# A hybrid decoder layer with 32 experts: key lengths as logarithms, another router order, ring places released in the mixer, last expert in smaller transfers

## What is computed

```python
h = layer_norm(x, ln0_g, ln0_b)
mix = token_mixer(h, mem, ...)            # projections, gated delta rule, short conv, cross-attention
h = layer_norm(ALPHA * h + mix, ln1_g, ln1_b)
ffn = moe_ffn(h, ...)                     # 32 experts, 4 per token
out = layer_norm(ALPHA * h + ffn, ln2_g, ln2_b)

# in token_mixer, the part of q and k that the change touches
q = l2_normalize(heads(q)) * GDN_HEAD_DIM ** -0.5
k = l2_normalize(heads(k))
o = gated_delta_rule_chunked(q, k, v, g, beta)
o = o * rsqrt(mean(square(o)) + RMS_EPS) * gdn_norm

# in moe_ffn
logits = x @ w_router + b_router
top_logits, top_idx = top_k(logits, 4); top_w = softmax(top_logits)
gate, up = split(x_e @ w_gate_up[e] + b_gate_up[e], 2)    # for the tokens of expert e
gate = min(gate, 7); up = clip(up, -7, 7)
y = ((up + 1) * gate * sigmoid(1.702 * gate)) @ w_down[e] + b_down[e]
out[token] += top_w * y
```

## Time and profile before

| | before |
|---|---|
| median of 3 runs | 1257.62 us |
| the profiled execution's own time | 1255.7 us |
| its span, first to last instruction | 1254.0 us |
| PE busy | 1213.0 us (97%) |
| DVE busy | 390.5 us (31%) |
| ACT busy | 243.5 us (19%) |
| POOL busy | 148.7 us (12%) |
| granted TensorE clock, mean | 0.994 |
| DMA over the span | 453.45 MB, mean 362 GB/s |

### The profile page before, as it was taken

The page is one execution under the profiler, slowest core; times in us unless marked ns, Lnnn a source line. Parts: engine busy times, 40 slices in busy tenths (PEclk is TensorE's granted clock), DMA queues, the critical chain, the costliest instruction groups (busy, mean ns, idle before and its releaser), DMA issues.

```text
span 1254.0 us, 17233 instructions
## 1 busy us (share of the span) xinstructions
PE 1213.0 (97%) x7155; PEld 613.1 (49%) x7155; DVE 390.5 (31%) x768; ACT 243.5 (19%) x402; POOL 148.7 (12%) x106
## 2 busy tenths in 40 slices
PE   8999999999999999999999999999999999999995
PEld 8999999998733333333333333333333333333332
DVE  6675633335522222222222222222222222222224
ACT  5764354544210000000000000000010000000001
POOL 7454323555100000000000000000000000000000
PEclk9999999999999999999999999999999999999999
DMA  9644231875899999999999999999999999999994
GB/s 335 221 148 143 70 136 67 330 292 201 353 409 429 428 429 428 427 429 429 429 428 429 429 429 428 429 428 430 428 429 427 427 427 428 429 427 428 428 427 198
DMA packets 53388, 453.45 MB, mean 362 GB/s; under 512 B 6925, under 2 KB 7002, under 8 KB 28762
## 3 DMA queue, kind: packets, MB, share of 16 engines
q1 hardware_dynamic: 53338, 452.71, 87.0%
HBM read 451.64 MB, written 1.05 MB: 361 GB/s over the span
## 4 chain that ended last, share of the span: by engine, by line
PE 78%; DMA 8%; SPq 5%; DVE 3%; ACT 3%; issue 2%; POOL 0%; DVEq 0%; ACTq 0%
PE bank L1419 29%; PE bank L1491 15%; DMA late<-in_w_gate_up_dram 8%; PE bank L1209 6%; SPq L807 5%; PE bank L1210 5%; PE bank L1211 5%; PE bank L1504 4%; PE bank L1390 4%; PE bank L1405 2%; PE bank L1479 1%; ACT late L1181 1%; ACT w_hi L1069 1%; PE bank L1499 1%; DMA raw<-in_w_mem_kv_dram 0%
## 5 line engine op out<-in xcount | busy, mean ns | idle before, releaser
L1419 PE MATMUL bank<-late 128*64 128x512 f32 x1536 | 343.5, 595 | 5.4 <-DMA late<-in_w_gate_up_dram 5.4
L1491 PE MATMUL bank<-late 128*64 128x512 f32 x1024 | 229.6, 601 | 6.0 <-ACT late L1181 6.0
L1419 PEld LDWEIGHTS bank<-late 128*64 128x64 f32 x1536 | 106.7, 137 | 223.2 <-issue 209.6
L1491 PEld LDWEIGHTS bank<-late 128*64 128x64 f32 x1024 | 71.3, 138 | 142.4 <-issue 128.6
L1209 PE MATMUL bank<-act_hi,w_hi 128*128 128x256 f32 x448 | 129.5, 289 | 1.9 <-DVE early L1699 1.4
L1210 PE MATMUL bank<-act_lo,w_hi 128*128 128x256 f32 x448 | 125.8, 281 | 0.0
L1211 PE MATMUL bank<-act_hi,w_lo 128*128 128x256 f32 x448 | 125.7, 281 | 0.0
L1834 DVE TENSOR_SCALAR late<-bank 128x512 f32<-128x512 f32 x32 | 22.1, 692 | 308.9 <-PE bank L1419 308.9
L1419 PE MATMUL bank<-raw,late 128*64 128x512 f32 x512 | 116.7, 598 | 1.5 <-DMA raw<-in_w_gate_up_dram 1.5
L770 POOL TENSOR_TENSOR w_lo<-raw,w_hi 128x1024 fp32r<-128x1024 f32 x33 | 81.9, 2483 | 102.1 <-ACT w_hi L1069 102.0
L1209 PEld LDWEIGHTS bank<-act_hi,w_hi 128*128 128x128 f32 x448 | 84.3, 188 | 4.1 <-DVE early L1699 2.0
(11 more groups left out here) (321 smaller groups left out, 1186.4 us busy)
## 6 DMA issues: line engine op xcount, KB each, us to landing
late<-in_w_gate_up_dram SPq DMA_DIRECT2D x96, 2048.0 KB, 37.1
late<-in_w_down_dram SPq DMA_DIRECT2D x64, 2048.0 KB, 36.5
raw<-in_w_gate_up_dram SPq DMA_DIRECT2D x32, 2048.0 KB, 35.2
raw<-in_w_in_dram SPq DMA_DIRECT2D x8, 2048.0 KB, 9.0
early<-in_w_in_dram SPq DMA_DIRECT2D x6, 2048.0 KB, 8.1
raw<-in_w_br_dram SPq DMA_DIRECT2D x3, 2048.0 KB, 7.6
raw<-in_w_mem_kv_dram SPq DMA_DIRECT2D x8, 512.0 KB, 11.2
raw<-in_w_o_dram SPq DMA_DIRECT2D x1, 2048.0 KB, 8.5
```

Of the source, the lines that this page charges most:

```text
L1419: ins = mm(bk[64 * c:64 * c + 64, :], x_slotT[:, k % 4, 64 * (k // 4):64 * (k // 4) + 64], w[:, kk, at + 512 * c:at + 512 * (c + 1)], star ...
L1491: ins = mm(ps[3][64 * c:64 * c + 64, :], hidT[:, kk, 64 * q:64 * q + 64], w[:, kk, c * 512:(c + 1) * 512], start=(q == 0 and kk == 0), sto ...
```

## The change

1. **Lengths through logarithms.** The step "lengths" goes. "norms" becomes the first step: 16 matmuls against one column of ones; the squares are made on POOL, one head at a time, behind the `qkv` units. ACT takes the logarithm of the keys' sums and exp(-0.5 log), which is folded into beta; half the logarithm is folded into the cumulated decay. q is left unscaled, and its length enters as an epsilon of the output's normalisation. `z` is projected last of the five groups, and "decay functions" stand behind the last `qkv`.
2. **Router order.** The router's tables move to a place of their own (loaded behind the branches), `x1T` becomes two tiles elsewhere, ACT evicts two blocks earlier, the first half of tile 0's logits is computed before tile 1 is turned, ranks and residuals are interleaved, the counts go to a bank of their own, item 0 starts on half its tokens, and all `keep_warm` calls behind the start go.
3. **Ring places.** Places 6 and 8 are filled once the branches' sums are done, and 9 and 11 no longer wait for residuals and one-hots.
4. **Last expert.** Chunk 2 comes in two transfers, chunk 3 in four (gate halves first), chunks 4 and 5 in two each, each waited for on its own; the last items' scatter matrix is turned in the middle of `down`.
5. **Last normalisation.** DVE only centres the halves and finishes one; PE multiplies the other three by a diagonal matrix of the reciprocal deviation and adds b, and ACT copies them out.

```diff
-    + [("in", c) for c in (C_Z, C_XC, C_GC, C_GB, C_QM)]
+    + [("in", c) for c in (C_XC, C_GC, C_GB, C_QM, C_Z)]
...
-    ["scalars", "decay", "norms", "lengths", "scores", "tokens"]
+    ["norms", "scalars", "decay", "scores", "tokens"]
...
+    order += [("qkv", 0), ("qkv", 1), ("ab", 0), ("qkv", 2), ("abT", 0)] + [("qkv", n) for n in range(3, 12)]
+    order += [("decay functions",), ("g", "norms")]
+    g = [s for s in GDN_STEPS if s not in ("norms", "scalars", "decay", "olen", "onorm")]
+    long = [(kind, n) for kind in ("xc", "gc", "gb", "qm", "z") for n in range(4)]
+    at = {("xc", 1): [("log decay",)], ("xc", 2): [("g", "scalars")], ("xc", 3): [("g", "decay")]}
...
             elif name == "norms":
                 act.wait_ge(g_pe, GP["norms"])
-                        ins = a.activation(inv_norm[:, t, 4 * n:4 * n + 4], ps[4 + 2 * t + n][:, 0::P], ACT.Sqrt,
+                a.activation(log_k, ps[5][:, 0:NPB].rearrange("p (t h) -> p t h", t=NT), ACT.Ln,
+                             bias=eps_rms[:, 0:1]).then_inc(g_act, 1)
+                act.wait_ge(g_act, GA["norms"] - 1)
+                a.activation(beta_k, log_k, ACT.Exp, scale=-0.5).then_inc(g_act, 1)
...
+                for n in range(2 * H):
+                    for t in range(NT):
+                        at = t * H + n % H
+                        ins = mm(ps[4 + n // H][:, at:at + 1], squares[:, n, t * P:(t + 1) * P], ones[:, 0:1], start=True, stop=True)
...
-            elif name == "lengths":
-                pe.wait_ge(g_dve, GD["norms"])
-                for n in range(2 * H):
-                    for t in range(NT):
-                        ins = mm(ps[4 + n // 2][:, (n % 2) * T + t * P:(n % 2) * T + (t + 1) * P],
-                                 spread(inv_norm, t, n), ident[:], start=True, stop=True)
...
+                if s[0] == "qkv" and 1 <= s[1] <= 2 * H:
+                    c = s[1] - 1
+                    pool.wait_ge(silu_done, c + 1)
+                    if c < H:
+                        for k in range(2):
+                            src = halves(qkvT[:, c, :])[:, :, 1 - k, :]
+                            ins = eng.tensor_tensor(halves(squares[:, c, :])[:, :, k, :], src, src, ALU.mult)
+                    else:
+                        ins = eng.tensor_tensor(squares[:, c, :], qkvT[:, c, :], qkvT[:, c, :], ALU.mult)
+                    ins.then_inc(squared, 1)
...
             for c in range(RAW):
                 raw_spent(sp, N_MIX - RAW + (c - N_MIX) % RAW)
                 chunk_dma(sp, c, w_gate_up[0, 0], w_down[0, 0], *ring_place(c)[0:2])
+                if c == 0:
+                    wait_sums(sp, KD)
+                    for m in BEHIND_BRANCHES:
+                        chunk_dma(sp, m - EC, w_gate_up[0, 1], w_down[0, 1], *ring_place(m)[0:2])
             sp.wait_ge(bank_full[bank_of(("wo", 1, 1))], turn_of(("wo", 1, 1)))
             for m in range(EC, RING):
-                if m == SPARE:
-                    continue
-                if m == SPARE - 1:
-                    sp.wait_ge(x1_added, 2 * NT)
-                if m == RING - 1:
-                    sp.wait_ge(onehots, 1)
-                chunk_dma(sp, m - EC, w_gate_up[0, 1], w_down[0, 1], *ring_place(m)[0:2])
+                if m != SPARE and m not in BEHIND_BRANCHES:
+                    chunk_dma(sp, m - EC, w_gate_up[0, 1], w_down[0, 1], *ring_place(m)[0:2])
...
                     if s == ("x1T", 1, 0):
-                        keep_warm(10, ps[7])
+                        logit_rows(0, range(4))
...
+            def logit_rows(t, ks):
+                u = ("logits", t)
+                bk = ps[bank_of(u)]
+                if ks.start == 0:
+                    pe.wait_ge(bank_free[bank_of(u)], turn_of(u) - 1)
+                    pe.wait_ge(router_in, 32)
+                for k in ks:
+                    if k % 4 == 0:
+                        h = ("x1T", t, k // 4)
+                        pe.wait_ge(bank_free[bank_of(h)], turn_of(h))
+                    ins = mm(bk[:, 0:NE], x1T[t][:, k, :], wr[:, k, :], start=(k == 0), stop=(k == KD - 1))
...
                 elif kind == "rank":
                     residual(0, 0)
+                    pe.wait_ge(r_mask, 1)
+                    mm(bk[:, 0:NE], before[:], mask[:, 0, :], start=True, stop=True)
+                    mm(bk[:, NE:2 * NE], ones[:], mask[:, 0, :], start=True, stop=False)
                     residual(0, 1)
                     pe.wait_ge(r_mask, 2)
...
-            residual(1, 0)
-            residual(1, 1)
             pe.wait_ge(bank_free[bank_of(("rank", 0))], turn_of(("rank", 0)))
             pe.wait_ge(onehots, 1)
             gather()
-            keep_warm(4, ps[3])
+            residual(1, 0)
             turn_tokens(0)
-            keep_warm(8, ps[3])
-            pe.wait_ge(ebias_in, 128)
             gate_up(0, item_places(0), first=True)
...
+        def last_chunk_dmas(sp, c, gu, dn, dst, landed):
+            if c == 3:
+                rows = gu[4 * P:8 * P, :].rearrange("(p k) n -> p k n", k=4)
+                to = dst.rearrange("p (k n) -> p k n", k=2)
+                for at, done in ((0, gate_parts_in), (FF, [up_part_in, landed])):
+                    for kk in range(2):
+                        sp.dma_start(to[:, kk, at:at + FF], rows[:, 2 + kk, at:at + FF]).then_inc(done[kk], 16)
...
+                    elif parts is not None and q == 3:
+                        for kk in range(2):
+                            pe.wait_ge(gate_parts_in[kk], parts)
+                            ins = rows_of(kk, 0)
+                        ins.then_inc(gate_done, 1)
+                        pe.wait_ge(up_part_in, parts)
+                        rows_of(0, FF)
+                        pe.wait_ge(landed, count)
+                        ins = rows_of(1, FF)
...
-                    d.scalar_tensor_tensor(out=o, in0=o, scalar=ln_rstd[:, t:t + 1],
-                                           in1=lnp2[:, 1, 512 * c:512 * c + 512], op0=ALU.mult, op1=ALU.add).then_inc(half_out, 1)
+                    centre(t, c).then_inc(centred, 1)
...
+            for t in range(NT):
+                act.wait_ge(centred, 2 * t + 1)
+                a.activation(diag[:, t, :], ident[:], ACT.Copy, scale=ln_rstd[:, t:t + 1]).then_inc(spread_out, 1)
+            for n, (t, c) in enumerate(SPREAD_BANKS):
+                act.wait_ge(scaled, n + 1)
+                a.copy(hx[:, t, 512 * c:512 * c + 512], SPREAD_BANKS[t, c][:, :]).then_inc(half_out, 1)
```

353 lines of the change are left out of this document (214 added, 139 removed).

## The result

The changed kernel took 1263.03 us (median of 8 runs, 1260.78 to 1266.79) where the kernel before took 1256.51 (8 runs, 1254.09 to 1257.86): ratio 1.0062, 95% interval 1.0052 to 1.0072. It is 0.6% slower, clear of the interval; I had forecast 1248.1, faster, within 1244.0 to 1254.0. The profiled execution took 1266.79 us with a span of 1264.9.

The account below looks back on a forecast made before the run. Prediction: PE bounds the mixer, DMA transfers the experts' stage, whose end hangs on when the ring's refill begins. Terms -4.0 - 1.8 - 2.6 - 1.15 = -9.5 gave 1248.1 us against 1257.6, range 1244.0 to 1254.0.

Parts of the forecast that it names:

- Part 1, mixer: Mixer up to the end of `wo`: removed matmuls and fewer table switches save 4.0 us, between 5.6 and 0.5.
- -3.6 for "lengths": Mixer: removing 16 matmuls that appear as 32 instructions, 3.57 us in a PE-bound stage, saves 3.6 us.
- The term for the tables: Mixer's `qkv` units: table switches go, saving half of a 0.8 us PE stall at 80 to 82 us, -0.4.
- The third rival: Mixer: POOL's twelve squares and DVE's `w_lo` hold each other up, +14.8 on the forecast, 1263 us, slower; chance 0.04.
- Part 2, router: From the end of `wo` to item 0: start 2.7 us sooner, 0.9 given back, -1.8; bounds -3.0 and +6.
- a rival of 0.13: Router: with 22 warming matmuls gone the clock falls through gather, residual, biases and chunk 0, about +6, 1254.1 us; chance 0.13.
- the 18.6 forecast: Router: item 0 would start 18.6 instead of 21.3 us behind the end of `wo`.
- Part 3, early fills: Ring places 6 and 8 filled at 301 us: first fill 7 to 9 us ahead of first release; own price 0.
- the releases change nothing: Ring: transfers 6 and 8 delay places 1 and 2 and fill no gap; only the mixer gains, 1249.9 us; chance 0.08.
- Part 4, last expert: Last expert: four instructions (0.9 us) instead of 16 (3.65) follow chunk 3's landing; -2.6, or -2.2 if chunk 5 is late.
- Part 5, last normalisation: End: DVE needs 3.9 us, PE's matmuls lie under ACT's work, fourth DMA goes out sooner, -1.15; bounds -1.6 and 0.

Follow-up runs that it names:

- the kernel with more distance: Changed kernel with scalars, decay, scores one unit later, tokens two units behind scores, sums against 128 columns and the router's warming products back: 1256.66 us, 1.0009.
- the kernel with the mixer of before and the padding: Changed kernel with the mixer change undone and the 10, 4 and 8 warming products put back in the router: 1254.42 us, 0.9999.
- the one with the other router order: Changed kernel with the first half of tile 0's router rows multiplied behind the turning of tile 1, no warming products: 1261.54 us, 1.0042.

## Why the prediction was wrong

**Part 1, mixer: -4.0 forecast, +7.6 in the profile, +6.3 in the medians.** The removed work was priced right. Two sentences of the prediction failed. "Each step has a whole unit of PE before its answer is needed, scores has two (5.6 us): 0" counted from decay to scores, and overlooked that tokens, which waits for the longest chain of DVE, had lost a unit: `xc` 2 had stood without a step between them. I had not added up that chain, 5.57 us by itself and 8.3 us from the end of PE's products at 102.9 to 111.16, against the 2.8 us of cover; PE waited 5.3 us. And "I price them as before ... loading the weights sets it": the 32 instructions did take 3.6 to 4.1 us, but I gave the one-column form no price in clock. It has one of 0.0024 of the time, 3.0 us, in the kernel before; in the kernel with more distance it was 0.0013, 1.6 us, with overlapping intervals, and in the changed kernel itself 128 columns gained nothing, since new waits took the place. In the profile: waits from 60 us to the end of `wo` 11.6 us instead of 7.3, and low stretches of 6.8, 6.8 and 3.4 us, in which a product takes 0.213 instead of 0.118 us. 1 - 0.118/0.213 is 45%, and 45% of 17 us, less the idle at their edges, is about 7 us. With 4.3 us more waits and -3.6 for "lengths" the sum is near +8. The term for the tables, -0.4, was about one stall: from 40 to 120 us ACT loads four tables in the changed kernel where it loaded eight, but three of the four now stand close together, from 76.8 to 82.0 us, ahead of scalars.

**The third rival** had the right mechanism and the wrong place. The squares were harmless: POOL took 0.62 and 0.51 us for them and PE waited for none. What was held were DVE's short instructions in the scores chain, by POOL's `w_lo`. Worse, had shown me POOL held by DVE and I did not ask which instructions of DVE stand on the path and can be held by POOL. The time that this rival gave, 1263, is the measured one by chance. The Trainium skill (SBUF — State Buffer, section "SBUF: two separate sides") says that DVE and POOL share a pair of ports under an exclusive lock, held for a whole instruction, and that of DVE's instructions it concerns those in a two-port mode and, where POOL's instruction reads SBUF, those with two inputs in SBUF. The runs agree: the 128x8 product with two SBUF inputs took 1.70 us and the SBUF copy of 128x16 took 2.35 us, both until POOL's end, and the pass with one input in a bank 1.40 us. I had cited this section for the squares and not asked which instructions of DVE it names.

**Part 2, router: -1.8 forecast, +4.8 in the profile.** The wait that I worked out is there: PE turns tile 1 only at 335.8, because L1344 ahead of it waits 3.36 us for the bank. What failed is the price of the removed padding, which I kept apart as a rival of 0.13. From 332 to 353 us the clock is 0.50, through just the four pieces that I had named: gather 3.68 instead of 1.94 us. For this execution +6 was a fair size (25.8 us instead of 18.6); by the ratios the padding is worth 0.9 and 1.6 us, and the whole of the changed router, fills and end, without padding, stands at +0.0012, 1.5 us. The path itself was priced right: with the padding and the mixer of before the gather starts 13.6 us behind `wo` (forecast 14.0), and without the last twelve padding products item 0 follows it after 4.55 us (forecast 4.6). Together that is 18.2 for the 18.6 forecast (18.3 when taken from the end of `wo` at 321.48; I had used 321.2); but no kernel here has both, and the sum took both. Whether the first ten products alone would give them was not tried.

**Part 3, early fills.** The mechanism was as forecast (fills at 307 us, share 0.07 at 345, first refill with item 0's first place), and the sixth place's refill does fix the end: from there to the last scatter all kernels need 871 to 875 us. But since parts 1 and 2 did not bring item 0 forward, the lead had nothing to serve; undone, it costs nothing that can be measured. The rival "the releases change nothing" was right in the outcome and wrong in the reason: the two transfers did fill a gap.

**Part 4, last expert: -2.6 forecast.** From the sixth place's refill to the last scatter the two profiles with the old end show 874.55 and 874.89 us, the eighteen with the new end 870.9 to 873.9, 872.7 on average: -2.0 (-0.7 in the changed kernel's own profile). The step that was mis-sized is "now four (0.9)" instructions behind the landing T: PE's 48 products run without a wait for rows from 1230.60 to the end. PE, not the landing, sets this stretch in the changed kernel. The turned scatter (0.44) also lies inside `down`, so from the last gate and up product to the last scatter it is 11.76 us where it was 11.78; the forecast had 11.85 there (12.75 less 0.9), so that part of it was right.

**Part 5, last normalisation: -1.15 forecast, -0.65 measured**, the same within 0.05 in every profile. From the first centred half the fourth transfer is issued at +5.6 us, where I had +4.9: PE's products wait 0.81 us, until 1258.33, for the first diagonal, which ACT ends at 1258.18, and then need 2.81 us for all six, so that they no longer lie under ACT's work: its last copy waits 0.27 us for them. The 2.0 us of part 4 and the 0.65 of part 5 are readings of profiles: by the ratio 0.9999 [0.9986, 1.0011] of the kernel with the mixer of before and the padding, parts 2 to 5 together bring at most 1.8 us.

**Slips in the sums.** Twelve squares of 1.2 us make 14.4 and not 14.8 us. The bounds named for the range add up to 3.3 us below and 6.5 above, 1244.8 to 1254.6 and not 1244.0 to 1254.0. The last DMA at 1250.35 instead of 1251.55 would be -1.2 and not -1.15. None of them changes the outcome.

## What to carry to other kernels

When a step is moved, write down for each waiting instruction how much work covers it before and after, and set against that the whole chain that it waits for, including what stands ahead in the answering engine's queue. Put short SBUF-only instructions of DVE behind the chain for which another engine waits, or keep POOL's long subtractions out of that stretch. In this kernel the first took 1.9 us off the wait at tokens, and the second 2.8 us with no distance added, of which 2.1 us show in the ratio, within overlapping intervals. Before removing products that do nothing, or shrinking products to one column, ask what the clock does behind them.

## What the hardware showed that I had not expected

A run of 32 products against one column, 3.6 us with PE busy throughout, was followed by a granted clock of 1.2 GHz for 3.4 to 7 us in seven of the eight profiled kernels that have them, with full products on both sides; none of the twelve with 128 columns showed it at that place. In the eighth, the one with the other router order, it came 12 us later, behind a wait of 1.9 us at scalars. Nor does the same wait always bring it: every kernel has a wait of 2.2 us between 295 and 304 us, and in twelve of the twenty profiles a low stretch of 3.4 us follows it; in eight, that of the kernel before among them, none does. So single profiles can differ by several microseconds with the same code. A DVE instruction of 128x16 elements, 0.18 us alone, took 2.35 us beside POOL.
